# First output projection of a two-layer trunk: six pairs by Strassen products; first chunk's product order and 16 constant matmuls for 20

## The chip, the cores and the metric

The kernel runs on one core of a Trainium2 chip, as one program. The metric is device microseconds of one execution; the kernel before has a median of 2319.4 us over 3 runs (2317.81 to 2319.68). Engines are named as in the profile: PE is the matrix engine (PEld its weight loads), DVE the vector engine, ACT the scalar engine, POOL GpSimd, SP the engine that issues most transfers.

## The reference, cut to what matters

One sequence of 512 tokens with 2048 features goes through two layers. All of it is fp32.

```python
for layer in range(DEPTH):                      # DEPTH = 2
    h = rms_norm(x, norm_pre[layer])
    y = ab_mixer(h, ...) if layer == 0 else conv_mixer(h, ...)   # both end in  y @ w_out, 2048 x 2048
    x = x + rms_norm(y, norm_post[layer])
    h = rms_norm(x, xattn_norm_pre[layer])
    y = memory_cross_attention(h, rms_norm(mem, mem_norm[layer]), ...)
    x = x + rms_norm(y, xattn_norm_post[layer])
```

The change concerns the last line of `ab_mixer`, `return y @ w_out`: a product of 512 x 2048 by 2048 x 2048.

## The kernel before, in words

**Layout.** Activations lie transposed, features on partitions: a tensor of 2048 x 512 is 16 tiles of 128 x 512. `X` (`residual`) holds the residual, `Y` and other scratch lie in `work`. A matmul of full fp32 accuracy is made of three passes: the input is split in a high and a low part (`H_hi`, `H_lo`, together `input_hi_lo`), a weight in `w_hi` and `w_lo`, and hi x hi, hi x lo and lo x hi are summed in PSUM.

**Chunks.** Weights come in chunks of 4 input tiles by 256 output features (128 x 1024, 512 KB). SP loads a chunk to one of 4 slots of `raw`; ACT rounds it to `w_hi` (`split`, L642); DVE subtracts to get `w_lo` (`split`, L1798); PE runs 24 matmuls of 512 columns on it (`chunk`, L1260 to L1262). Four chunks make one pair of output tiles. Counters order all of this: `lo_ready` (weights split), `chunk_used` (PE done with a chunk), `acc_free` (PSUM banks read out).

**First output projection.** `out_phase(0, C_OUT0, P_OUT0, 4)` runs 8 pairs, 32 chunks, with an input split by `split_input` from `X`. The residual `x`, whose place the mixer's result has taken, is loaded again right after that split (16 transfers on semaphore `reloaded`, on SP ahead of the fifth chunk). Sums of squares of each output tile go through ACT and POOL; then `norm(0)` computes the norm, adds the residual and starts the opening of the cross-attention's query projection (`opening`, L1610 to L1623), for which PE waits.

**Strassen pairs.** The second layer's input projection (28 pairs) and output projection (6 of its 8 pairs, `wino_out`) do not use chunks but Winograd's form of Strassen's algorithm: a pair of output tiles takes 7 products instead of 8, each over 8 input tiles and 256 tokens. A product runs 8 matmuls of 512 columns (high and low input side by side, L1757) and 8 of 256 columns (low weights, L1762). Its operands are quarters of the weights and sums of quarters: A11, A12, A22 come from SP by transfer; S1 and S3 from POOL by adding transfers (`wino_sums`, L2807 and L2809); S2 and S4 by DVE additions (`weight_sum`, L2503 and L2506). Sums of input tiles are made beforehand by DVE (`turned_sums_out`, L2688 to L2693), their highs by ACT (L1159), their lows by DVE (`turned_low_out`, L2703). Products are read out of PSUM by DVE and ACT (`evacuate_product`, L2571 to L2598), which PE waits for in products 4 to 7 of a pair. The stage works so: 2 pairs by chunks, meanwhile the input sums; `take_out` copies the two chunk pairs out (L2713, in the first layer L2248); then six pairs by products; meanwhile, in the last pair, the residual returns from DRAM (L610, L613), and `norm(2)` and `opening` follow.

**Start.** While the first transfers are under way, PE runs 20 matmuls on a constant (L1234); then `ab_round(0, 0)` begins with chunk 0.

Of the kernel before, what the change touches and what calls it, by code (L numbers as in the profile page):

```python
# [50 lines left out]
C_Q0, P_Q0 = C_OUT0 + 32, P_OUT0 + 8  # L51
# [138 lines left out]
S_PAIRS, OUT_PAIRS = 28, 6  # L190
S_CHUNKS = 7 * S_PAIRS
S_ALL = 7 * (S_PAIRS + OUT_PAIRS)
# [8 lines left out]
def run_of(q):  # L201

    return (0, S_PAIRS, C_C) if q < S_PAIRS else (S_PAIRS, S_PAIRS + OUT_PAIRS, C_OUT1 - 8)


def s_slot(i):

    return (i + 2) % S_SLOTS
# [11 lines left out]
def build(nc, books, dram):  # L220
    ctx = ExitStack()
    with ctx:
# [19 lines left out]
        gate_pair = sb("gate_hi_lo", KT * 32, F32R)  # L242
        gate_half = lambda n: gate_pair.rearrange("p (k a n) -> p k a n", a=2, n=16)[:, :, n, :]
# [95 lines left out]
        s_s3 = lambda q: raw[:, CW:2 * CW] if q in (0, S_PAIRS) else raw_s3[:, :]  # L339
        home = {"A11": "r0", "S2": "r0", "S1": "r2", "A12": "r1", "S4": "r1", "A22": "r3"}  # L340
        s_source = lambda q, name: s_s3(q) if name == "S3" else s_raw[home[name]][q % 2]
# [5 lines left out]
        fourths_out = lambda b: Y[:, 4 * T:6 * T].rearrange("p (k n) -> p k n", n=HT) if b else four(Y, 8, 0)  # L347
        sq_out = lambda k: (Y[:, (14 + k % 2) * T:(15 + k % 2) * T] if k < 12 else cq[:, (k % 2) * T:(k % 2 + 1) * T])
        out_corner = lambda n, f, h: Y[:, (2 * n + f) * T + h * HT:(2 * n + f) * T + (h + 1) * HT]
        corner = lambda q, f, h: corner_of(q % 4, f, h) if q < S_PAIRS else out_corner(q - S_PAIRS + 2, f, h)  # L350
        before_first, before_second, before_third = (lambda b, k=k, t=t: four(t, 4 * b + k, 1) for k, t in ((0, X), (8, X), (0, Y)))

        def moving(q, pos, kt):

            if pos in (1, 2, 4):
                third = turned_y if q < S_PAIRS else turned_o
# [27 lines left out]
        params_in, consts_in, tables_in, gate_in, reloaded, out_done = (  # L384
            sem(n) for n in ("params_in", "consts_in", "tables_in", "gate_in", "reloaded", "out_done"))
# [38 lines left out]
        def _(sp):  # L424
# [86 lines left out]
            for n in range(8):  # L511
                load_pair(dram["ab_w_out"], 4 * n, C_OUT0 + 4 * n)
                if n == 0:
                    for k in range(KT):
                        sp.wait_ge(*ZV(f"lo{k}"))
                        sp.dma_start(xt(k), dram["x"][k]).then_inc(reloaded, 16)

            def cross_loads(l):
                for c in range(4 * l, 16):
# [4 lines left out]
            cross_loads(0)  # L524
            conv_sections = (0, 2, 1, 3)
            for c in range(16):
                j, kt0 = opening_chunk(c)
                load(dram["c_w_in"], 32 * conv_sections[j] + kt0 // 4, C_C + c)
                if c in (9, 11):
                    for k in range(8 * (c // 11), 8 * (c // 11) + 8):  # L530
                        sp.wait_ge(*(NG(f"x{k}", 1) if k > 1 else NV(f"x{k}", 1)))
                        sp.dma_start(dram["x_kept"][k], xt(k)).then_inc(x_kept, 16)

            def s_load(q, at, home_, sem_):

                if q < S_PAIRS:
                    w, block = dram["c_w_in"], 4 * (8 * conv_sections[q % 4] + q // 4 + 1) + at
                else:
                    w, block = dram["c_w_out"], 4 * (q - S_PAIRS + 2) + at
                sp.dma_start(home_, w[P * block:P * (block + 1), :]).then_inc(sem_, 16)  # L540

            def s_loads(q):

                first, _, base = run_of(q)
# [18 lines left out]
                if q == 0:  # L563
                    sp.wait_ge(*CM("o3", 0))
# [5 lines left out]
                s_load(q, 1, s_raw["r1"][q % 2], s_in["r1", q % 2])  # L570
# [3 lines left out]
                if q:  # L574
                    sp.wait_ge(s_lo, 7 * q)
                s_load(q, 3, s_raw["r3"][0], a22_in)

            def after_pairs(end, c):

                q = end - 2 + c % 2  # L580
                sp.wait_ge(s_lo, 7 * q + (5 if c < 2 else 3))
# [2346 lines left out]
```

## Time and profile before

| | us |
|---|---|
| median of 3 runs | 2319.4 (2317.81 to 2319.68) |
| profiled execution, its own time | 2319.7 |
| span of its profile, first to last instruction | 2317.7 |
| first output projection, `norm(0)`, opening (984.46 to 1212.13) | 227.67 |
| second output projection, `norm(2)`, opening (1975.05 to 2193.22) | 218.17 |

The profile's times count from its first instruction; 2.0 us lie around the span. Stages are bounded by the start of their first matmul. A busy time of PE counts overlapping matmuls once, so a stage's length and the waits ahead of a matmul say more than the share.

### The profile page before, as it was taken

Reading aid. Unit: us, or ns where it says so; the run is one execution under the profiler, and the core shown is the slowest. Engines: PE = TensorE matmul, PEld = TensorE weight load, DVE = VectorE, ACT = ScalarE, POOL = GpSimd, SP = SyncE. Lnnn points to the kernel's source line nnn. Section 1 sums busy time; section 2 is a strip of 40 time slices with the busy share of each in tenths; the row PEclk is TensorE's granted clock in tenths of the full one; section 3 lists DMA queues with packets and bytes.
Section 4 is the critical chain, followed back from the end, with each engine's and each line's share of the span. In section 5 each row is a group of like instructions: output and inputs, shape, how many; then the busy total and the mean of one; then the engine's idle time right before and its main releaser. Section 6 shows DMA issues by size and latency. Waiting matters only on the chain.

```text
span 2317.7 us, 31681 instructions
## 1 busy us (share of the span) xinstructions
PE 2287.0 (99%) x12237; PEld 1919.2 (83%) x12237; DVE 1647.6 (71%) x2240; ACT 985.3 (43%) x1618; POOL 293.8 (13%) x225
## 2 busy tenths in 40 slices
PE   9999999999999999999999899999999999999998
PEld 7888888888787778888877788888888888888776
DVE  6676767664455658643385699888988898988855
ACT  5333333323343437532243364444444444544444
POOL 4000000001010101001040340000000000122400
PEclk9999999999999999999999999999999999999999
DMA  5322222223322224442322245766676666466322
GB/s 209 98 78 82 77 81 77 82 79 99 109 91 73 89 67 156 160 167 84 115 64 72 83 146 172 200 193 190 191 198 179 188 181 201 145 188 204 114 64 91
DMA packets 99553, 297.89 MB, mean 129 GB/s; under 512 B 18624, under 2 KB 21856, under 8 KB 99424
## 3 DMA queue, kind: packets, MB, share of 16 engines
q1 hardware_dynamic: 89152, 258.89, 33.1%
q0 software_dynamic: 9792, 35.66, 8.8%
q8 instruction: 86, 1.41, 0.2%
q10 hardware_dynamic: 480, 1.59, 0.2%
q14 instruction: 43, 0.35, 0.0%
HBM read 285.06 MB, written 11.03 MB: 128 GB/s over the span
## 4 chain that ended last, share of the span: by engine, by line
PE 91%; DVE 5%; issue 2%; ACT 1%; DMA 1%; POOL 0%; DVEq 0%; ACTq 0%; SPq 0%; POOLq 0%
PE acc L1260 15%; PE acc L1262 14%; PE acc L1261 14%; PE m L1757 12%; PE acc L1757 6%; PE m L1762 6%; PE acc L1762 3%; PE acc L1618 2%; PE acc L1619 2%; PE acc L1623 2%; DVE weights_lo L1798 1%; PE m L1434 1%; PE m L1442 1%; ACT weights_hi L642 1%; PE m L1650 1%
## 5 line engine op out<-in xcount | busy, mean ns | idle before, releaser
L1260 PE MATMUL acc<-input_hi_lo,weights_hi 128*128 128x512 f32 (+1 forms) x1696 | 670.8, 395 | 0.8 <-DVE input_hi_lo L2667 0.3
L1262 PE MATMUL acc<-input_hi_lo,weights_lo 128*128 128x512 f32 (+1 forms) x1696 | 648.3, 382 | 0.0
L1261 PE MATMUL acc<-input_hi_lo,weights_hi 128*128 128x512 f32 (+1 forms) x1696 | 647.4, 382 | 0.0
L1798 DVE TENSOR_TENSOR weights_lo<-weights_raw,weights_hi 128x1024 fp32r<-128x1024 f32 x264 | 359.8, 1373 | 134.9 <-ACT weights_hi L642 134.1
L1260 PEld LDWEIGHTS acc<-input_hi_lo,weights_hi 128*128 128x128 f32 x1696 | 319.2, 188 | 72.8 <-issue 14.8
L1262 PEld LDWEIGHTS acc<-input_hi_lo,weights_lo 128*128 128x128 f32 x1696 | 318.8, 188 | 63.9
L1261 PEld LDWEIGHTS acc<-input_hi_lo,weights_hi 128*128 128x128 f32 x1696 | 319.5, 188 | 57.3 <-issue 1.9
L642 ACT ACTIVATE weights_hi<-weights_raw 128x1024 fp32r<-128x1024 f32 x264 | 274.5, 1058 | 144.1 <-PE acc L1262 108.9
L1757 PE MATMUL m<-input_hi_lo,weights_hi 128*128 128x512 f32 x816 | 205.5, 394 | 3.1 <-issue 2.0
L1757 PEld LDWEIGHTS m<-input_hi_lo,weights_hi 128*128 128x128 f32 x816 | 146.6, 189 | 31.3 <-issue 3.9
L1026 ACT ACTIVATE weights_hi<-weights_raw 128x1024 fp32r<-128x1024 f32 x104 | 110.0, 1059 | 112.6 <-PE m L1762 51.9
L2495 DVE TENSOR_TENSOR weights_lo<-weights_raw,weights_hi 128x1024 fp32r<-128x1024 f32 x104 | 128.0, 1231 | 37.6 <-ACT weights_hi L1026 37.6
L2752 POOL TENSOR_TENSOR small<-small 128x4 f32<-128x4 f32 (+1 forms) x19 | 24.5, 1288 | 835.5 <-DVE small L2038 371.6
L1762 PEld LDWEIGHTS m<-input_hi_lo,weights_lo 128*128 128x128 f32 x816 | 111.2, 190 | 8.4 <-DVE weights_lo L2495 0.4
L1762 PE MATMUL m<-input_hi_lo,weights_lo 128*128 128x256 f32 x816 | 113.8, 282 | 0.0
L2495 DVE TENSOR_TENSOR weights_lo<-work,weights_hi 128x1024 fp32r<-128x1024 f32 x68 | 86.6, 1274 | 13.5 <-ACT weights_hi L1026 13.5
L2828 POOL TENSOR_TENSOR work<-work 128x512 f32<-128x512 f32 x42 | 61.0, 1453 | 275.0 <-ACT work L939 197.8
L1026 ACT ACTIVATE weights_hi<-work 128x1024 fp32r<-128x1024 f32 x68 | 71.7, 1055 | 36.9 <-DVE work L2506 36.9
L2807 POOL DMA_DIRECT2D weights_s<-in_c_w_in x27 | 23.7, 879 | 479.8 <-DMA weights_s<-in_c_w_in 479.8
L1618 PE MATMUL acc<-input_hi_lo,weights_hi 128*128 128x512 f32 x180 | 73.5, 408 | 6.6 <-DVE input_hi_lo L2281 6.6
L2838 POOL TENSOR_TENSOR residual<-residual,work 128x512 f32<-128x512 f32 x42 | 71.0, 1713 | 50.9 <-DVE work L2274 50.9
L1619 PE MATMUL acc<-input_hi_lo,weights_lo 128*128 128x512 f32 x180 | 72.7, 404 | 0.0
(403 smaller groups left out, 3638.8 us busy)
## 6 DMA issues: line engine op xcount, KB each, us to landing
weights_raw<-in_ab_w_in SPq DMA_DIRECT2D x126, 512.0 KB, 3.6
weights_raw<-in_c_w_in SPq DMA_DIRECT2D x73, 512.0 KB, 4.5
work<-in_c_w_in SPq DMA_DIRECT2D x42, 512.0 KB, 3.7
weights_raw<-in_m_w_kv SPq DMA_DIRECT2D x32, 512.0 KB, 3.7
weights_raw<-in_ab_w_out SPq DMA_DIRECT2D x32, 512.0 KB, 4.4
weights_raw<-in_m_w_q SPq DMA_DIRECT2D x32, 512.0 KB, 3.6
weights_raw<-in_c_w_in POOLq DMA_DIRECT2D x29, 512.0 KB, 7.5
weights_s<-in_c_w_in SPq DMA_DIRECT2D x27, 512.0 KB, 3.8
```

The source lines that it names most:

```text
L642: act.activation(w_hi[:, s * CW:(s + 1) * CW], raw[:, c * CW:(c + 1) * CW], ACT.Copy)\
L1026: act.activation(w_hi[:, s * CW:(s + 1) * CW], s_source(q, name), ACT.Copy).then_inc(s_hi, 1)
L1260: pe.matmul(out, w_hi[:, o:o + P], hi(kt), start=kt == first_kt, stop=False)
L1261: pe.matmul(out, w_hi[:, o:o + P], lo(kt), start=False, stop=False)
L1262: last = pe.matmul(out, w_lo[:, o:o + P], hi(kt), start=False, stop=kt == last_kt)
L1618: pe.matmul(bank(p0 + n, j), w_hi[:, o:o + P], H_hi[:, x], start=kt == 0, stop=False)
L1619: pe.matmul(bank(p0 + n, j), w_lo[:, o:o + P], H_hi[:, x], start=False, stop=False)
L1757: pe.matmul(out.rearrange("p (a n) -> p a n", a=2), w_hi[:, o:o + P], moving(q, pos, kt)[0], start=kt == 0 and pos in S_FRESH, stop=False, ...
L1762: last = pe.matmul(high_half(out), w_lo[:, o:o + P], moving(q, pos, kt)[1], start=False, stop=kt == 7, skip_group_check=True)
L1798: TTO(w_lo[:, s * CW:(s + 1) * CW], raw[:, c * CW:(c + 1) * CW], w_hi[:, s * CW:(s + 1) * CW].bitcast(F32), ALU.subtract).then_inc(lo_read ...
L2495: TTO(w_lo[:, s * CW:(s + 1) * CW], s_source(q, name), w_hi[:, s * CW:(s + 1) * CW].bitcast(F32), ALU.subtract)\
L2838: pool.tensor_tensor(xt(k), xt(k), yt(k), ALU.add).then_inc(*NG.did(f"x{k}"))
```

## The change

The six last pairs of the first output projection are computed by Strassen products with the code of the second one (`wino_out(r, ...)` is now shared by r = 0 and r = 2, with one function on PE, ACT and DVE each). For that `w_out` is laid out on the host as halves of pairs, the run of products is numbered from 0 (6 here, then 28, then 6), and places are found for quarters where the memory keys and values (`mk`, `mv`) still lie: A12 of even pairs and A22 go to `Y`; from the fifth pair on A22 goes to the place of S1, once S2 has been summed (`late_fourth`). The residual is loaded again late, in the last pair (`residual_back`), no longer ahead of the fifth chunk. In `turned_sums_out` DVE now waits for its first sum before the second, for r = 2 too.

Apart from that, the first chunk of all runs two high products ahead of the low ones and starts before its low weights are there (`first_chunk`), behind 16 constant matmuls.

```diff
-            for k in range(20):
+            for k in range(16):
                 early = pe.matmul(M[3], gate_pair[:, 0:P], gate_pair[:, :], start=True, stop=True)
...
+            def first_chunk():
+                for kt in range(4):
+                    x = slice(kt * T, (kt + 1) * T)
+                    o = [kt * 256 + j * P for j in range(2)]
+                    if kt == 0:
+                        pe.wait_ge(hi_ready, 1)
+                    pe.wait_ge(*SA(f"hi{kt}"))
+                    for j in range(2):
+                        pe.matmul(acc[j][:, :], w_hi[:, o[j]:o[j] + P], H_hi[:, x], start=kt == 0, stop=False)
+                    pe.wait_ge(*SV(f"lo{kt}"))
+                    for j in range(2):
+                        pe.matmul(acc[j][:, :], w_hi[:, o[j]:o[j] + P], H_lo[:, x], start=False, stop=False)
+                    if kt == 0:
+                        pe.wait_ge(lo_ready, 1)
+                    for j in range(2):
+                        last = pe.matmul(acc[j][:, :], w_lo[:, o[j]:o[j] + P], H_hi[:, x], start=False, stop=False)
+                last.then_inc(chunk_used, 1)
...
-S_PAIRS, OUT_PAIRS = 28, 6
+S_FIRST = (0, 6, 34, 40)
+S_BASE = (C_OUT0 - 8, C_C, C_OUT1 - 8)
...
+        def s_home(q, r):
+            if run_of(q) == 0 and r == "r1" and q % 2 == 0:
+                return Y[:, 14 * T:16 * T]
+            if run_of(q) == 0 and r == "r3":
+                return s_raw["r2"][q % 2] if q >= 4 else Y[:, 12 * T:14 * T]
+            return s_raw[r][q % 2]
...
+            def late_fourth(q):
+                sp.wait_ge(s_lo, 7 * q + 3)
+                sp.wait_ge(s_sum["S2"], q + 1)
+                s_load(q, 3, s_home(q, "r3"), a22_in)
...
+            def residual_back(r, c):
+                w, sems = ((dram["x"], (reloaded, reloaded2)) if r == 0 else (dram["x_kept"], (x_back, x_back2)))
+                sp.wait_ge(s_used, 7 * (S_FIRST[r + 1] - 1) + (5 if c else 3))
+                for k in range(8 * c, 8 * c + 8):
+                    sp.dma_start(xt(k), w[k]).then_inc(sems[c], 16)
...
-            for n in range(8):
-                load_pair(dram["ab_w_out"], 4 * n, C_OUT0 + 4 * n)
-                if n == 0:
-                    for k in range(KT):
-                        sp.wait_ge(*ZV(f"lo{k}"))
-                        sp.dma_start(xt(k), dram["x"][k]).then_inc(reloaded, 16)
+            for n in range(2):
+                load_pair(dram["ab_w_out"], 4 * n, C_OUT0 + 4 * n)
+            for q in range(S_FIRST[1]):
+                s_loads(q)
+                if q >= 5:
+                    late_fourth(q - 1)
+            for c in (0, 2):
+                after_pairs(S_FIRST[1], c)
...
+            late_fourth(5)
+            residual_back(0, 0)
+            after_pairs(S_FIRST[1], 1)
...
+            residual_back(0, 1)
+            after_pairs(S_FIRST[1], 3)
...
             def turned_sums_out(r, b):
...
                 TTO(four(third_out, 4 * b, 1), high1, low1, ALU.subtract).then_inc(turn_in, 1)
+                dve.wait_ge(turn_in, 8 * r + 4 * b + 1)
                 TTO(before_first(b), low0, low1, ALU.subtract).then_inc(turn_in, 1)
...
-            out_phase(0, C_OUT0, P_OUT0, 4, lambda kt: ZV(f"lo{kt}", 0))
+            wino_out(0, C_OUT0, P_OUT0, (0, 4, 8, 12), lambda kt: ZV(f"lo{kt}", 0))
             norm(0)
...
-              "ab_w_out": by_block(np.asarray(ab_w_out)[0]), "c_w_in": by_quarter(np.asarray(c_w_in)[0]),
+              "ab_w_out": halves_of_pairs(np.asarray(ab_w_out)[0]), "c_w_in": by_quarter(np.asarray(c_w_in)[0]),
```

On PE, at the program's start, these rows stand in the kernel before (names are those of the tiles, out first; the number behind x counts equal instructions):

```order
L1234 MATMUL m<-gate_hi_lo 128x512 x20
L1260 MATMUL acc<-input_hi_lo,weights_hi 128x512
L1261 MATMUL acc<-input_hi_lo,weights_hi 128x512
L1262 MATMUL acc<-input_hi_lo,weights_lo 128x512
L1260 MATMUL acc<-input_hi_lo,weights_hi 128x512
```

and these after the change:

```order
L1271 MATMUL m<-gate_hi_lo 128x512 x16
L1288 MATMUL acc<-input_hi_lo,weights_hi 128x512 x2
L1291 MATMUL acc<-input_hi_lo,weights_hi 128x512 x2
L1295 MATMUL acc<-input_hi_lo,weights_lo 128x512 x2
L1288 MATMUL acc<-input_hi_lo,weights_hi 128x512 x2
```

The first matmul on the low weights has moved from the third to the fifth place behind the constant ones.

On SP, from the first output projection's loads to those of the next projection, the kernel before has

```order
L434 DMA weights_raw<-in_ab_w_out 128x1024 x4
L516 DMA residual<-in_x 128x512 x16
L434 DMA weights_raw<-in_ab_w_out 128x1024 x28
L434 DMA weights_raw<-in_m_w_q 128x1024 x16
```

and the changed one, from the first quarters of its sixth pair on (L537 loads quarters, L446 chunks of the query projection, L595 the residual),

```order
L537 DMA weights_raw<-in_ab_w_out 128x1024 x2
L537 DMA weights_a_52<-in_ab_w_out 128x1024
L537 DMA weights_s_53<-in_ab_w_out 128x1024
L537 DMA weights_raw<-in_ab_w_out 128x1024
L446 DMA weights_raw<-in_m_w_q 128x1024 x2
L537 DMA weights_raw<-in_ab_w_out 128x1024
L595 DMA residual<-in_x 128x512 x8
L446 DMA weights_raw<-in_m_w_q 128x1024
L595 DMA residual<-in_x 128x512 x8
L446 DMA weights_raw<-in_m_w_q 128x1024 x13
```

The residual has moved from the stage's start to its end, and the query projection's fourth chunk stands behind all of it. The two single `weights_raw<-in_ab_w_out` rows are the late A22 of the fifth and sixth pair.

On DVE, where the first chunk pair is read out, the changed kernel has (L1860 splits weights, L2610 to L2616 are the input sums, L2637 reads out a pair, L2626 makes lows)

```order
L1860 TENSOR_TENSOR weights_lo<-weights_raw,weights_hi 128x1024 x2
L2637 COPY work<-acc 128x512 x2
L2610 TENSOR_TENSOR work<-residual 128x4x256
L2612 TENSOR_TENSOR residual<-residual 128x4x256
L2614 TENSOR_TENSOR residual<-residual 128x4x256
L2616 TENSOR_TENSOR work<-residual 128x1024
L1860 TENSOR_TENSOR weights_lo<-weights_raw,weights_hi 128x1024
L2626 SCALAR_TENSOR_TENSOR turned_third_out<-work,turned_third_out 128x4x256
```

where the kernel before had only the copies (L2248) and the weights' splits (L1798): the second half of the input sums and the lows now stand between the copies and the splits of the seventh and eighth chunk.

## Rows read from the trace of the kernel before

**Rows 1.** The page, parts 1 and 4: busy time, and the chain by engine.

```profile
PE 2287.0 (99%) x12237; PEld 1919.2 (83%) x12237; DVE 1647.6 (71%) x2240; ACT 985.3 (43%) x1618; POOL 293.8 (13%) x225
...
PE 91%; DVE 5%; issue 2%; ACT 1%; DMA 1%; POOL 0%; DVEq 0%; ACTq 0%; SPq 0%; POOLq 0%
```

**Rows 2.** Windows by stage: length, engines' busy time, granted clock, DMA share, GB/s.

```profile
984.46:1159.58 175.12, 175.12 (x780) 145.13 (x778) 64.04 (x60) 47.73 (x58) 18.64 (x15) 1.00 0.36 122
1159.58:1166.17 6.59, 3.06 (x26) 2.81 (x24) 2.89 (x6) 1.23 (x2) 1.02 (x1) 0.90 0.00 0
1166.17:1212.13 45.96, 45.96 (x191) 37.80 (x192) 40.52 (x42) 25.02 (x37) 23.70 (x14) 0.94 0.26 81
1975.05:2018.66 43.61, 43.61 (x192) 36.12 (x193) 41.38 (x44) 22.84 (x30) 5.38 (x4) 1.00 0.42 125
2018.66:2040.83 22.17, 20.25 (x113) 17.23 (x112) 19.41 (x24) 11.05 (x14) 4.84 (x4) 1.00 0.67 174
2040.83:2138.70 97.87, 97.87 (x563) 86.02 (x562) 83.67 (x105) 46.89 (x61) 25.16 (x18) 1.00 0.66 193
2138.70:2148.21 9.51, 5.28 (x35) 4.88 (x33) 5.32 (x9) 2.75 (x5) 1.03 (x1) 0.62 1.05 404
2148.21:2193.22 45.01, 45.01 (x192) 36.94 (x192) 40.51 (x42) 25.04 (x37) 23.68 (x14) 0.97 0.29 96
```

**Rows 3.** PE's timeline, second output projection: sixth and seventh product of its first pair.

```profile
2033.61 2.08 PE L1757 MATMUL m<-input_hi_lo,weights_hi 128*128 128x512 f32 x8 [0.82 <-DVE fifth L2576]
...
2037.96 2.09 PE L1757 MATMUL m<-input_hi_lo,weights_hi 128*128 128x512 f32 x8 [1.09 <-issue]
```

**Rows 4.** Windows of the input projection's first two Strassen pairs, columns as in Rows 2.

```profile
1422.98:1443.64 20.66, 19.78 (x114) 17.26 (x113) 18.66 (x24) 11.32 (x14) 1.79 (x2) 1.00 0.69 195
1443.64:1463.21 19.57, 19.57 (x114) 17.20 (x113) 16.27 (x22) 8.46 (x10) 1.77 (x2) 1.00 0.70 188
```

**Rows 5.** Timelines of DVE and POOL: start, length, operation, idle time ahead.

```profile
1006.56 1.29 DVE L2248 COPY work<-acc 128x512 f32<-128x512 f32 x2 [4.95 <-PE acc L1262]
...
1998.54 1.28 DVE L2713 COPY work<-acc 128x512 f32<-128x512 f32 x2
...
2030.32 1.21 DVE L2506 TENSOR_TENSOR work<-work,weights_raw 128x1024 f32<-128x1024 f32 x1
...
2033.04 0.42 DVE L2576 TENSOR_TENSOR fifth<-m,fifth 128x256 f32<-128x256 f32 x1
...
2037.43 0.43 DVE L2584 SCALAR_TENSOR_TENSOR work<-m,fifth 128x256 f32<-128x256 f32 x1
...
2049.35 2.32 DVE L2506 TENSOR_TENSOR weights_a<-weights_a,weights_raw 128x1024 f32<-128x1024 f32 x1
...
2048.78 1.81 POOL L2828 TENSOR_TENSOR work<-work 128x512 f32<-128x512 f32 x1 [0.47 <-ACT work L1166]
```

**Rows 6.** ACT's timeline: the first pair's S1, and the query chunk split in `norm(2)`.

```profile
2020.92 1.06 ACT L1026 ACTIVATE weights_hi<-weights_raw 128x1024 fp32r<-128x1024 f32 x1 [2.75 <-DMA weights_raw<-in_c_w_out]
...
2151.34 1.05 ACT L642 ACTIVATE weights_hi<-weights_raw 128x1024 fp32r<-128x1024 f32 x1
```

**Rows 7.** Timelines of PE and DVE at the program's start.

```profile
1.47 7.72 PE L1234 MATMUL m<-gate_hi_lo 128*128 128x512 f32 x20 [1.47 <-DVE gate_hi_lo L1802]
9.28 0.50 PE L1260 MATMUL acc<-input_hi_lo,weights_hi 128*128 128x512 f32 x1
...
14.85 0.39 PE L1260 MATMUL acc<-input_hi_lo,weights_hi 128*128 128x512 f32 x1
...
7.13 0.75 DVE L1807 SCALAR_TENSOR_TENSOR input_hi_lo<-residual,parameters,input_hi_lo 128x512 fp32r<-128x512 f32 x1 [5.71 <-ACT input_hi_lo L655]
8.00 1.23 DVE L1798 TENSOR_TENSOR weights_lo<-weights_raw,weights_hi 128x1024 fp32r<-128x1024 f32 x1
```

**Rows 8.** Transfers: quarters with median us to landing; SP's timeline, the residual's issues.

```profile
work<-in_c_w_out SPq DMA_DIRECT2D x9, 512.0 KB, 3.7
...
2133.30 4.33 SPq L613 DMA_DIRECT2D residual<-residual_kept  x8
```

More of the change, by code:

```diff
@@ L587, in _ @@
+            for q in range(S_FIRST[1], S_FIRST[2]):
+                s_loads(q)
+                n, j = divmod(q - S_FIRST[1], 4)
+                if j == 2 and n < 4:
                     sp.wait_ge(*WV("y", n))
@@ L1066, in conv_first @@
                             turned_high(HIGHS_AT[c], n)
-                for i in range(S_SLOTS):
+                for i in range(CONV_I, CONV_I + S_SLOTS):
                     s_split(i)
@@ L1205, in _ @@
-            wino_out()
+            wino_out(2)
             norm(2)
@@ L1718, in last_projection @@
                         turned(k)
-            out_phase(0, C_OUT0, P_OUT0, 4, lambda kt: ZV(f"lo{kt}", 0))
-            norm(0)
-            cross(0, 0)
-            norm(1)
-            def conv_group(n, first=False):
-                if first:
-                    opening(1, C_C, P_C)
-                for c in range(8 if first else 0, 16):
-                    chunk(C_C + c, P_C + c // 4, 4 * (c % 4), KT - 1, n=n,
-                          between=(lambda k: next_rms(1, c, k)) if first else None)
-            conv_group(0, first=True)
             def wino_product(q, pos):
@@ new lines, in _, with turned_sums @@
+            split_input(0, xt, C_OUT0, 8)
+            wino_out(0)
+            norm(0)
+            cross(0, 0)
+            norm(1)
+            def turned_sums(b):
+                (low0, low1), (high0, high1) = ([four(X, 4 * b + k, h) for h in range(2)] for k in (0, 8))
+                dve.wait_ge(turn_scaled, 8 * (b + 1))
+                TTO(before_third(b), high1, low1, ALU.subtract).then_inc(turn_in, 1)
+                TTO(before_first(b), low0, low1, ALU.subtract).then_inc(turn_in, 1)
+                dve.wait_ge(turn_in, 8 + 4 * b + 2)
+                TTO(before_second(b), high1, before_first(b), ALU.add).then_inc(turn_in, 1)
+                dve.wait_ge(turn_in, 8 + 4 * b + 3)
+                TTO(fourths(b), before_second(b), high0, ALU.subtract).then_inc(turn_in, 1)
@@ new lines, in turned_low @@
+            def turned_low(b):
+                for n in (2, 0, 1):
+                    of = (before_first, before_second, before_third)[n](b)
+                    home_, k = (turned_y if n == 2 else turned_x), 4 * b + (0, 8, 0)[n]
+                    dve.wait_ge(turn_hi, 8 + 3 * b + (2, 0, 1).index(n) + 1)
+                    STT(out=four(home_, k, 1), in0=of, scalar=-1.0 if n == 1 else 1.0,
+                        in1=four(home_, k, 0).bitcast(F32), op0=ALU.mult, op1=ALU.subtract).then_inc(turn_lo, 1)
@@ L2841, in _ @@
                 if r == 1:
-                    for q in range(S_PAIRS):
+                    for q in range(S_FIRST[1], S_FIRST[2]):
                         wino_sums(q)
```

571 lines of the change are left out of this document (290 added, 281 removed).

## The prediction

> **What bounds the kernel now.** I read the profile's page first: PE is busy for 99% of the span and carries 91% of the chain that ended last [rows 1]. So a stage lasts as long as its matmuls follow each other plus the waits ahead of them, and an edit off PE counts only where PE comes to wait for it. Then I cut both output projections into windows by stage [rows 2]; they are the same product of the same size, one by chunks and one by Strassen pairs, so the second is a measured model of what the first is to become. In the first, eight chunk pairs take 175.12 us (21.89 each, PE without a gap), the norm 6.59 and the opening of the query projection 45.96: together 227.67. In the second, two chunk pairs take 43.61, the first Strassen pair 22.17, the other five 97.87 (19.57 each), the norm 9.51 and the opening 45.01: together 218.17.
>
> Next I looked for what makes the first Strassen pair longer than the others by 22.17 - 19.57 = 2.60 us. PE's timeline shows it: the sixth product waits 0.82 us for DVE's second addition for the fifth term (L2576), the seventh 1.09 [rows 3], the rest being gaps too short to be listed as waits. DVE's row L2576 ends at 2033.46, just ahead of the sixth product, and its row L2584 at 2037.86, just ahead of the seventh [rows 5]. DVE is late there because that pair's S1 came late: ACT split it only at 2020.92, after 2.75 us of waiting for its transfer [rows 6], and from then on DVE works through splits, additions and the second copy without rest. The input projection's first pair loses less: 20.66 - 19.57 = 1.09 us [rows 4].
>
> **The change part by part.**
>
> *Six pairs by products.* Six of the eight pairs go from 21.89 to 19.57 us. With the second projection's parts put in for the first's, the stage is 43.61 + 6 x 19.57 + 9.51 + 45.01 = 215.55 plus what the first pair waits. Against 227.67 that is a gain of 12.12 us less that wait. The longer norm (9.51 for 6.59) is inside the sum: 24 columns of sums of squares now follow the last product, where the old loop put 8 of them between the last chunk's matmuls; and the opening is 0.95 us shorter in the second projection, at a granted clock of 0.97 for 0.94 [rows 2]. I take both as they stand, since the changed kernel has the same steps in the same order there.
>
> *The first pair's wait.* It lies between nothing, as in the five pairs that follow, and the model's 2.60; the input projection's first pair, with 1.09, stands between. Which is nearest? The chain to S1 starts where DVE has copied out the first chunk pair and makes the second half of the input sums. In the first projection that copy came 1006.56 - 984.46 = 22.10 us after the stage's first matmul, in the second 1998.54 - 1975.05 = 23.49 [rows 5], because DVE had a backlog there from the step before. So the chain can start 1.4 us earlier. Not all of that arrives at S1: in the first projection ACT's third high waits for all four sums, so that the squares that POOL adds ahead of its weight sums come about 1 us later than in the model, and the transfers share the engines (0.67 of them busy in that window [rows 2]). I take 1.1 us of the 1.4, hence a wait of 1.5 us.
>
> *DVE and POOL beside each other.* In the Strassen pairs DVE makes its additions while POOL adds squares. The row for S4 shows what that costs: 1.21 us at 2030.32, and 2.32 at 2049.35, while POOL's addition runs from 2048.78 for 1.81 [rows 5]. So an overlapped addition loses 1.11 us, and with two POOL additions a pair DVE loses some 2.2; it has 19.57 - 83.67 / 5 = 2.84 us free in a pair with these losses already in it [rows 2], so PE loses nothing. The Trainium skill's page "SBUF — State Buffer" (section "SBUF: two separate sides") speaks against the change here: a VectorE operation with two SBUF inputs and a GpSimd operation that reads SBUF take the same port pair as an exclusive lock, and the later one waits for the whole of the other. Two full waits of 1.81 in place of 1.11 would take 1.4 us more from DVE's free 2.84, so by that rule too the sum stays as it is.
>
> *A22 at a new place, and late for two pairs.* For the first four pairs A22 is asked for as in the model. For the fifth and sixth it takes the place of S1, so SP may ask for it only when S1 has been split and S2 summed. One product is 19.57 / 7 = 2.80 us; I estimate 3 us from the pair's start for that. With the median landing of 3.7 us for such quarters [rows 8] it is there at 6.8. Its split is needed by the seventh product, at 6 x 2.80 = 16.8, so about 15.7 would still do. Cost nothing, covered by some 9 us; behind it on SP stand the query chunks and the residual, which are not needed before the norm.
>
> *The residual's return.* It now competes with nothing at the stage's start, where PE waited for nothing anyway; worth nothing. At the end it returns as in the model, where transfers fill the engines through the norm (1.05, 404 GB/s [rows 2]). Two things differ: the 1 MB of gain rows of the model is not loaded here, and the query projection's fourth chunk stands behind the last eight residual tiles. In the model SP issues those eight from 2133.30 for 4.33 us [rows 8]; the chunk would follow at 2137.7 and land, at 404 GB/s behind 2 MB of them, by about 2145. ACT splits it at 2151.34 in the model [rows 6]. Cost nothing, covered by 6 us; if that cover were gone, ACT's highs for the opening would be queued behind it and PE would wait for them.
>
> *One more wait on DVE in the shared sums*, for r = 2 too: it keeps two additions of the last block from overlapping by about 0.1 us each, on the same chain to S1. Between 0 and 0.3; I take 0.15 lost.
>
> *The first chunk.* PE ends the 20 constant matmuls at about 9.0 and starts chunk 0 at 9.28, when DVE's low weights, 1.23 us from 8.00, are done; chunk 1 starts at 14.85, so 24 matmuls take 5.57, 0.232 each [rows 7]. DVE begins these low weights at 8.00 because the high ones are ready then, and the first input's low part is done at 7.13 + 0.75 = 7.88. With 16 constant matmuls PE is free at about 8.1, four matmuls of the first tile fit ahead of 9.28, and 20 are left: 9.28 + 20 x 0.232 = 13.92, a gain of 0.93. The third tile's low part comes just in time, for which I take off 0.1: 0.85. Bounds: 0 if PE meets a wait later that absorbs it, 1.15 if all from 8.1 on is used. PE is without longer gaps from there to the projection, so I let the gain run through.
>
> Sum: 12.12 - 1.5 - 0.15 + 0.85 = 11.3 us. Against the profiled execution's 2319.7 that is 2308.4; this execution lay 0.3 above the median, so I forecast **2308.1 us**.
>
> **The rivals.**
>
> *The first pair waits as in the model, and the first chunk's gain is small.* For it: the chain to S1 is bound by transfers, which do not care for DVE's earlier start. Against: the copy's 1.4 us. Time: 12.12 - 2.60 - 0.3 + 0 to 0.85 = 9.2 to 10.1 gained, 2309.3 to 2310.2. Chance 0.25.
>
> *A transfer is late.* Either A22 in the last two pairs, if it lands more than 9 us after my estimate, or the fourth query chunk or the residual after the norm. For it: the queue is fuller than in the model's pairs, and POOL's adding transfers go through the same engines. Against: 6 and 9 us of cover. Four us of lateness on A22 count twice: 2316; a chunk late by 3 us gives 2311. Chance 0.12.
>
> *DVE becomes the bound of the Strassen pairs: slower.* Each pair has 2.84 us of DVE to spare; the stage's gain is about 2 us a pair. From 2.84 + 2.02 = 4.9 us more of DVE a pair the change costs time. That needs five more of its some nine long operations a pair to be stretched by 1.11 us. If all nine were, a pair took some 26 us and the kernel 2347. For it: overlapped additions do double. Against: POOL is busy for 25.16 of 97.87 us in the model [rows 2], and the changed stage has the same POOL work. Chance 0.04. (It is what the rule of the Trainium skill's page "SBUF — State Buffer", named above, would come to if every long operation met one of POOL's.)
>
> *The pairs gain nothing,* because halves of 256 columns run no better here than chunks: 2319. Against: 19.57 us a pair both in the second output projection's last five and in the input projection's second [rows 2, 4]. Chance 0.04.
>
> **How the numbers follow.** The forecast case has 0.55. The range 2305.8 to 2312.0 holds it with its bounds (no wait in the first pair and a first chunk of 1.15 give 13.27 us and 2306.1; I add 0.3 for the spread between executions), all of the second case and a third of the late transfers: some 0.85. A measurement of this kernel can tell about 0.2%, 4.6 us, from no change. Faster by more than that (below 2314.8): the first two cases and most of the third, 0.91. Same: 0.05. Slower: 0.04.
>
> **What would show it.** In the changed kernel's profile, Strassen pairs two to six of the first projection should take 19.6 us each, the first one 20.5 to 22, PE's wait there ahead of the sixth or seventh product and named after DVE; the norm some 9.5 us and the opening 45. Chunk 1 should start near 13.9. The prediction is wrong if PE waits ahead of a seventh product in the fifth or sixth pair (A22), if ACT waits for a transfer in `norm(0)`, or if DVE is busy through whole pairs.

## The result, and the profile after

The changed kernel takes 2307.4 us (median of 5 runs, 2307.04 to 2309.31), the kernel before beside it 2319.7 (5 runs): a ratio of 0.995, 95% interval 0.9936 to 0.9964. The forecast was 2308.1, the range 2305.8 to 2312.0. The total is right; in the profile two of its terms came out smaller than forecast, and the account below weighs them against the scatter between profiles.

The profile after: span 2305.5, 12.24 us less than before. The stage windows that answer to [rows 2] (times, then busy times of PE, PEld, DVE, ACT and POOL, granted clock, DMA share, GB/s): the first output projection's two chunk pairs, first Strassen pair, other five, norm and opening, the stretch from there to the next opening; then the second projection's first pair and its other five.

```profile
983.88:1027.51 43.63, 43.63 (x195) 36.13 (x194) 36.26 (x36) 20.62 (x26) 6.26 (x5) 1.00 0.46 144
1027.51:1049.39 21.88, 20.24 (x113) 17.23 (x112) 18.64 (x23) 11.09 (x14) 4.58 (x4) 1.00 0.60 165
1049.39:1147.25 97.86, 97.86 (x562) 86.00 (x561) 83.78 (x105) 46.70 (x60) 24.52 (x18) 1.00 0.66 191
1147.25:1156.77 9.52, 5.32 (x34) 4.93 (x33) 5.31 (x9) 2.96 (x5) 1.03 (x1) 0.62 0.94 367
1156.77:1201.70 44.93, 44.93 (x192) 36.91 (x192) 40.44 (x42) 25.04 (x37) 23.60 (x14) 0.97 0.26 82
1201.70:1320.51 118.81, 112.74 (x514) 91.50 (x513) 72.13 (x80) 45.77 (x82) 21.53 (x17) 0.97 0.24 76
...
2006.91:2028.64 21.73, 20.26 (x114) 17.23 (x113) 19.09 (x24) 11.15 (x14) 4.40 (x4) 1.00 0.66 177
2028.64:2126.50 97.86, 97.86 (x562) 86.01 (x561) 83.65 (x105) 46.55 (x60) 24.95 (x18) 1.00 0.65 192
```

The one stretch of before that [rows 2] lack:

```profile
1212.13:1331.90 119.77, 113.70 (x514) 92.48 (x513) 72.13 (x80) 45.77 (x82) 21.51 (x17) 0.96 0.24 75
```

So the 12.24 us are made of: 0.58 at the start (the stage begins at 983.88 for 984.46); 9.85 in the stage, 217.82 for 227.67 (pairs 175.12 to 163.37, norm 6.59 to 9.52, opening 45.96 to 44.93); 0.96 in the stretch behind it (119.77 to 118.81), which the change does not touch; and 0.85 in what remains, 0.44 of it in the second projection's first pair (22.17 to 21.73).

PE's timeline in the first pair shows the model's two waits again, ahead of the sixth and the seventh product:

```profile
1042.18 2.09 PE L1804 MATMUL m<-input_hi_lo,weights_hi 128*128 128x512 f32 x8 [0.55 <-DVE fifth L2579]
...
1046.52 0.70 PE L1804 MATMUL m<-input_hi_lo,weights_hi 128*128 128x512 f32 x2 [1.09 <-issue]
```

DVE's first copy, POOL's timeline to S1's issue (L2878 is S3's adding transfer, L2880 S1's), ACT's split of S1 and DVE's low split of it:

```profile
1005.95 1.29 DVE L2637 COPY work<-acc 128x512 f32<-128x512 f32 x2 [4.51 <-PE acc L1318]
...
1013.85 1.72 POOL L2899 TENSOR_TENSOR work<-work,squares 128x512 f32<-128x512 f32 x1 [22.30 <-ACT squares L1096]
1015.71 2.10 POOL L2899 TENSOR_TENSOR work<-work,rstd_rows 128x512 f32<-128x512 f32 x1
1017.75 1.05 POOL L2878 DMA_DIRECT2D weights_raw<-in_ab_w_out  x1
1018.50 1.22 POOL L2880 DMA_DIRECT2D weights_raw<-in_ab_w_out  x1
...
1029.49 1.06 ACT L1053 ACTIVATE weights_hi<-weights_raw 128x1024 fp32r<-128x1024 f32 x1 [4.11 <-DMA weights_raw<-in_ab_w_out]
...
1030.58 1.23 DVE L2551 TENSOR_TENSOR weights_lo<-weights_raw,weights_hi 128x1024 fp32r<-128x1024 f32 x1 [3.94 <-ACT weights_hi L1053]
```

The copy comes 22.07 us after the stage's first matmul, as forecast; S3 is issued 33.87 after it, S1's split starts at 45.61. In the second projection of before these were 23.49, 34.03 and 45.87 (S3's issue there at 2009.08, the rest from [rows 5, 6]): of the 1.4 us gained at the copy 0.2 to 0.3 reach S1 in this profile. DVE is idle for 3.94 us ahead of S1's low split, so it is S1, and not S3 (split at 1024.32) or DVE's own earlier work, that DVE waits for.

At the start PE's timeline reads

```profile
8.21 0.73 PE L1288 MATMUL acc<-input_hi_lo,weights_hi 128*128 128x512 f32 x2 [0.67 <-ACT weights_hi L676]
8.78 0.63 PE L1291 MATMUL acc<-input_hi_lo,weights_hi 128*128 128x512 f32 x2
9.47 0.73 PE L1295 MATMUL acc<-input_hi_lo,weights_lo 128*128 128x512 f32 x2
...
14.33 0.39 PE L1316 MATMUL acc<-input_hi_lo,weights_hi 128*128 128x512 f32 x1
```

Four matmuls stand ahead of the low weights, as forecast, but these came at 9.47 (9.28 in [rows 7]), since the first input landed later in this execution: ACT's first high starts at 6.49 (6.30 before).

### The profile page after: what moved, and what is told of

Read it like the earlier page. It is cut to its first block, busy times and chain, and to the rows that moved or that the text cites. A ratio compares the mean times of both kernels' runs of the same rounds, so it can differ in the third digit from the quotient of the medians.

```text
span 2305.5 us, 32170 instructions
## 1 busy us (share of the span) xinstructions
PE 2271.9 (99%) x12329; PEld 1911.9 (83%) x12329; DVE 1724.5 (75%) x2346; ACT 1018.2 (44%) x1662; POOL 308.6 (13%) x237
## 3 DMA queue, kind: packets, MB, share of 16 engines
q0 software_dynamic: 11520, 41.95, 10.4%
## 4 chain that ended last, share of the span: by engine, by line
PE 88%; DVE 6%; issue 2%; ACT 2%; DMA 1%; POOL 1%; DVEq 0%; ACTq 0%; SPq 0%; POOLq 0%
PE m L1804 14%; PE acc L1316 13%; PE acc L1318 12%; PE acc L1317 12%; PE acc L1804 7%; PE m L1809 7%; PE acc L1809 4%; PE acc L1677 2%; PE acc L1678 2%; PE acc L1682 2%; DVE weights_lo L1860 1%; PE m L1490 1%; PE m L1498 1%; ACT weights_hi L676 1%; PE m L1709 1%
## 5 line engine op out<-in xcount | busy, mean ns | idle before, releaser
L1316 PE MATMUL acc<-input_hi_lo,weights_hi 128*128 128x512 f32 (+1 forms) x1504 | 595.9, 396 | 0.7 <-DVE input_hi_lo L2797 0.3
L1318 PE MATMUL acc<-input_hi_lo,weights_lo 128*128 128x512 f32 (+1 forms) x1504 | 573.6, 381 | 0.0
L1317 PE MATMUL acc<-input_hi_lo,weights_hi 128*128 128x512 f32 (+1 forms) x1504 | 572.7, 381 | 0.0
L1860 DVE TENSOR_TENSOR weights_lo<-weights_raw,weights_hi 128x1024 fp32r<-128x1024 f32 x240 | 324.3, 1360 | 84.3 <-ACT weights_hi L676 83.6
L1316 PEld LDWEIGHTS acc<-input_hi_lo,weights_hi 128*128 128x128 f32 x1504 | 283.2, 188 | 64.8 <-issue 14.8
L1318 PEld LDWEIGHTS acc<-input_hi_lo,weights_lo 128*128 128x128 f32 x1504 | 282.7, 188 | 56.4
L1317 PEld LDWEIGHTS acc<-input_hi_lo,weights_hi 128*128 128x128 f32 x1504 | 283.5, 188 | 49.8 <-issue 1.9
L1804 PE MATMUL m<-input_hi_lo,weights_hi 128*128 128x512 f32 x960 | 241.5, 393 | 4.4 <-issue 3.1
L1804 PEld LDWEIGHTS m<-input_hi_lo,weights_hi 128*128 128x128 f32 x960 | 172.6, 189 | 37.4 <-issue 6.4
L2822 POOL TENSOR_TENSOR small<-small 128x4 f32<-128x4 f32 (+1 forms) x19 | 24.5, 1290 | 822.8 <-DVE small L2100 371.6
L1809 PE MATMUL m<-input_hi_lo,weights_lo 128*128 128x256 f32 x960 | 134.0, 282 | 0.0
L2878 POOL DMA_DIRECT2D weights_s<-in_c_w_in x27 | 23.6, 872 | 480.1 <-DMA weights_s<-in_c_w_in 480.1
L1804 PE MATMUL acc<-turned_first,weights_hi 128*128 128x512 f32 x320 | 80.1, 392 | 0.0
L1804 PE MATMUL m<-turned_first,weights_hi 128*128 128x512 f32 x320 | 80.1, 392 | 0.0
L1804 PE MATMUL acc<-input_hi_lo,weights_hi 128*128 128x512 f32 x320 | 80.1, 392 | 0.0
L1677 PE MATMUL acc<-input_hi_lo,weights_hi 128*128 128x512 f32 x180 | 73.3, 408 | 6.7 <-DVE input_hi_lo L2343 6.7
```

What stands on the lines that cost most here:

```text
L1316: pe.matmul(out, w_hi[:, o:o + P], hi(kt), start=kt == first_kt, stop=False)
L1317: pe.matmul(out, w_hi[:, o:o + P], lo(kt), start=False, stop=False)
L1318: last = pe.matmul(out, w_lo[:, o:o + P], hi(kt), start=False, stop=kt == last_kt)
L1677: pe.matmul(bank(p0 + n, j), w_hi[:, o:o + P], H_hi[:, x], start=kt == 0, stop=False)
L1804: pe.matmul(out.rearrange("p (a n) -> p a n", a=2), w_hi[:, o:o + P], moving(q, pos, kt)[0], start=kt == 0 and pos in S_FRESH, stop=False, ...
L1809: last = pe.matmul(high_half(out), w_lo[:, o:o + P], moving(q, pos, kt)[1], start=False, stop=kt == 7, skip_group_check=True)
```

## The experiments

All but one are edits of the changed kernel. First pairs and starts are read from the profiles, whose resolution the medians do not have.

**Both weight sums ahead of the squares** (POOL, both output projections).

```diff
-                    if r in (0, 2) and k == 2:
+                    if r in (0, 2) and k == 0:
                         wino_sums(S_FIRST[r])
```

> Edit: on POOL, in both output projections, the first pair's two weight sums (S3, S1) stand ahead of the first two additions of squares, no longer behind them. Theory 'queue' (the first pair waits because S1's adding transfer is issued behind POOL's two additions, which wait for ACT's squares and those for DVE's input sums): S3 is issued as soon as its base quarter has landed, near 1005 in place of 1017.75, S1 as soon as its own has, near 1016.8 in place of 1018.5, and without S3 ahead of it lands near 1022 to 1024 in place of 1029.5; the first pairs shrink from 21.88 and 21.73 to 19.6 to 20.6 us, the kernel gains 2 to 4 us more: 2303.5 to 2305.5. Theory 'transfers' (the transfer engines set the landing, whatever the issue): S1 lands within 1 us of where it did, first pairs 21.4 or more, kernel 2306.5 to 2308. Theory 'DVE' (its own backlog of splits and lows sets the wait): S1 lands early but the pairs stay above 21.2 us.

2304.4 us (5 runs, 2303.22 to 2305.63; ratio to before 0.9936, interval 0.9923 to 0.995). Windows of the two first pairs:

```profile
1027.29:1046.84 19.55, 19.55 (x113) 17.19 (x112) 18.07 (x23) 10.33 (x13) 5.50 (x4) 1.00 0.65 176
2004.46:2024.01 19.55, 19.55 (x113) 17.22 (x112) 17.94 (x23) 11.40 (x14) 5.76 (x5) 1.00 0.63 163
```

POOL's timeline, and ACT's split of S1:

```profile
1005.19 1.06 POOL L2878 DMA_DIRECT2D weights_raw<-in_ab_w_out  x1 [13.87 <-DMA weights_raw<-in_ab_w_out]
1016.96 0.88 POOL L2880 DMA_DIRECT2D weights_raw<-in_ab_w_out  x1 [10.71 <-DMA weights_raw<-in_ab_w_out]
...
1025.91 1.06 ACT L1053 ACTIVATE weights_hi<-weights_raw 128x1024 fp32r<-128x1024 f32 x1 [5.95 <-DMA weights_raw<-in_ab_w_out]
```

The wait is gone in both projections: the pairs take what the later ones take. DVE's backlog alone falls as a cause, since its work is the same. But S1 came only 1.5 us earlier to its issue and 3.6 earlier to its split, at 1025.91, later than the 1022 to 1024 that 'queue' had forecast: the issue is not all of it.

**S3 alone ahead of the squares**, S1 behind them as before.

```diff
-                    if r in (0, 2) and k == 2:
-                        wino_sums(S_FIRST[r])
+                    if r in (0, 2) and k in (0, 2):
+                        wino_sums(S_FIRST[r], (k // 2,))     # part 0: S3, part 1: S1
```

> The changed kernel with only S3 of the first pair ahead of POOL's two additions of squares; S1 stays behind them. Moving both gave first pairs of 19.55 us, but with that S1 was issued 1.5 us earlier and its landing took 8.9 us in place of 11.0. If the place behind the squares is what made PE wait: S1 issued near 1018 again, first pairs 20.5 us or more. If S3's half megabyte ahead of S1 in the transfer queue is what made it late: S1 lands 8 to 9 us after its issue, near 1026.5, first pairs 19.5 to 20.2.

POOL's issue of S1 and ACT's split of it:

```profile
1017.52 0.90 POOL L2883 DMA_DIRECT2D weights_raw<-in_ab_w_out  x1
...
1024.19 1.06 ACT L1053 ACTIVATE weights_hi<-weights_raw 128x1024 fp32r<-128x1024 f32 x1 [4.34 <-DMA weights_raw<-in_ab_w_out]
```

First pairs 19.55 and 19.55, with S1 issued behind the squares again, 6.67 us ahead of its split; in the changed kernel that distance is 10.99, and 9.7 to 10.4 in three other profiles with this code unchanged. So S1 is late because S3's transfer starts right ahead of it; the squares matter in that they hold S3 back until S1's base is there too. Whether the two delay each other by the order of their queue or by sharing the engines was not separated. Nor is it shown why S1's distance was 8.95 us with both sums ahead, where S3 was as early as here. Timed as a run of its own:

> The changed kernel with S3 alone ahead of POOL's additions of squares, timed. Its one look gave first pairs of 19.55 us and 2304.06; if that is the whole of the first pairs' waits, 2303.3 to 2305, the same as with both sums ahead (2304.44), and 2.5 to 4 us under the changed kernel's 2307.42.

2304.5 us (5 runs, 2303.92 to 2306.39; ratio 0.9935, interval 0.9921 to 0.9948), first pairs 19.55 again. Either order of POOL beats both kernels, the changed one by 3 us with no run in common.

**The seventh chunk's low split ahead of the input sums** (DVE).

```diff
-                turned_sums_out(r, 1)
                 split(c0 + 6)
+                turned_sums_out(r, 1)
```

> Edit: on DVE, in both output projections, the seventh chunk's low split stands ahead of the second half of the input sums, no longer behind it; POOL as it was. The base quarter of S1 is asked for some 4.9 us earlier (near 1008.4 for 1013.3), the input sums come 1.2 us later. Theory 'queue' (POOL's additions of squares, behind the input sums, hold S1 back): S1 is issued some 1.2 us later than now (near 1019.7) and lands no earlier than 1029; first pairs 21.6 to 23 us. Theory 'transfers' (late base quarters and their traffic hold S1 back): S1 lands 2 us or more earlier, first pairs 19.6 to 20.8.

S1 issued at 1019.36, split at 1028.51; first pairs 21.21 and 21.49, below the range of 'queue' and above that of 'transfers'. The early base quarter does not free the pair. Counted from the stage's start S1 was split 0.7 us earlier than in the changed kernel, although it was issued 1.1 later; but three profiles whose code is unchanged here show 0.6, 0.7 and 1.3 us earlier too, so a part of the quarters' traffic in the wait is not shown.

**The added DVE wait only for r = 0.**

```diff
-                dve.wait_ge(turn_in, 8 * r + 4 * b + 1)
+                if r == 0:
+                    dve.wait_ge(turn_in, 8 * r + 4 * b + 1)
```

> Edit: DVE's added wait between its first and second input sum only in the first output projection, in the second as before the change. The second projection's first pair took 22.17 us before the change and 21.73 with it. If the wait costs what the prediction gave it (0.15 us on the chain to S1): 21.5 to 21.65. If the wait is what made that pair shorter: 22.1 to 22.3. If both numbers are scatter of the transfers from execution to execution: anything from 21.4 to 22.4, with S1's issue at the same distance from the stage's start within 0.2 us.

21.97 us; and the first projection's first pair, whose code is untouched, 21.33 for 21.88. The scatter of these pairs (below) is larger than the effect that was looked for. S1's issue tells more: without the added wait it comes 34.62 us after the stage's first matmul, as in the kernel before (34.63), and with it 34.86 to 35.09 in five profiles. So the wait costs 0.2 to 0.5 us at S1's issue; at S1's split (45.69, beside 45.43 to 46.21 in those five) this is lost in the scatter.

**The first chunk alone**, put in the kernel before.

> The kernel before with the first chunk's new order and 16 constant matmuls alone. If the first chunk's gain runs through: chunk 1 starts 0.5 to 0.75 us ahead of 14.85, the first output projection starts as much ahead of 984.46, and the kernel gains 0.5 to 0.8 us: 2318.6 to 2319.2 beside 2319.4. If a later wait absorbs it: 0 to 0.2. The 0.96 us that the changed kernel gained between the opening and the second norm (the granted clock fell later there, in the norm before the next projection): if it comes from the Strassen stage's end, that stretch stays at 119.8 us here; if it varies from execution to execution, it may show 118.8 here too.

Chunk 1 starts at 14.28 (14.85 before), and the rows stay 0.6 to 0.7 us ahead up to the first norm. In this execution that norm took 7.51 us, beside 6.59 in the kernel before, whose code there is the same; the opening behind it began 0.2 us later than before. The opening takes 45.96 us, as in the kernel before, and the stretch behind it 119.67 (119.77 before). Norm and stretch:

```profile
1158.84:1166.35 7.51, 3.98 (x26) 3.63 (x24) 2.89 (x6) 1.23 (x2) 1.02 (x1) 0.66 0.00 0
1212.31:1331.98 119.67, 113.60 (x514) 92.49 (x513) 72.02 (x80) 45.64 (x82) 21.54 (x17) 0.96 0.25 75
```

The granted clock of the norm is 0.66, in the kernel before 0.90 [rows 2]. The median is 2318.5 (11 runs) for 2319.6; ratio 0.9996, interval 0.9987 to 1.0005: a time can't tell the first chunk's gain.

**20 constants with the new order; 16 with the old order; and a further order** in which the second tile's highs fill the wait for the low weights (with POOL's early sums).

```diff
-            for k in range(16):
+            for k in range(20):
                 early = pe.matmul(...)
```

> The changed kernel with 20 constant matmuls again, the first chunk's new order kept. If the gain of 0.5 to 0.6 us needs both parts: PE ends the constants at 9.0, goes straight on with 24 matmuls, chunk 1 starts at 14.5 to 14.7. If the order alone brings it: 14.2 to 14.35.

> The changed kernel with the old order of the first chunk behind 16 constant matmuls. If the low weights' readiness sets the start: the first matmul waits to 9.3 to 9.5 and chunk 1 starts at 14.8 to 15.1, no gain or a small loss. If the granted clock falls in the wait of nearly 2 us: matmuls of 0.43 us, chunk 1 after 15.5.

> Both weight sums ahead of the squares, as in the earlier run, and in the first chunk the second tile's two high products ahead of the first tile's low-weight products, which wait for DVE. Chunk 1 starts 0.2 to 0.35 us earlier than with the changed kernel's order (13.85 to 14.05 beside 14.03 to 14.33), first pairs 19.55 both, the kernel 2303.5 to 2305 beside 2304.4 for the sums alone; if the second tile's input lows then wait instead, no gain at the start.

PE's timelines at the start, of the 20 constants, the old order and the further order:

```profile
1.47 6.55 PE L1271 MATMUL m<-gate_hi_lo 128*128 128x512 f32 x20 [1.47 <-DVE gate_hi_lo L1864]
8.13 0.72 PE L1288 MATMUL acc<-input_hi_lo,weights_hi 128*128 128x512 f32 x2
...
14.25 0.39 PE L1316 MATMUL acc<-input_hi_lo,weights_hi 128*128 128x512 f32 x1
```

```profile
9.47 0.50 PE L1316 MATMUL acc<-input_hi_lo,weights_hi 128*128 128x512 f32 x1 [1.46 <-DVE weights_lo L1857]
...
15.06 0.39 PE L1316 MATMUL acc<-input_hi_lo,weights_hi 128*128 128x512 f32 x1
```

```profile
11.80 0.73 PE L1290 MATMUL acc<-input_hi_lo,weights_hi 128*128 128x512 f32 x2 [0.15 <-DVE input_hi_lo L1880]
...
14.20 0.39 PE L1327 MATMUL acc<-input_hi_lo,weights_hi 128*128 128x512 f32 x1
```

Fewer constants alone gain nothing (15.06 for 14.85, the low weights 0.19 later). The order alone brings the gain where the 20 constants end in time; they did here, at 8.02, while in the kernel before they ended at 9.19 [rows 7], because matmuls took up their fast pace earlier: from 5.3 to 6.4 us six of them run, in the kernel before four (the granted clock reads 1.00 in both, so the pace is read from the count). Sixteen keep the gain in either case. The further order trades the wait at 9.3 for one at 11.8 for DVE's third input low and gains nothing: 2305.8 us (5 runs), no better than the early sums by themselves and above the forecast 2303.5 to 2305. That low part is the next bound of the start.

**Two and four more DVE operations a pair** (r = 0; low splits made twice).

```diff
                 dve.wait_ge(s_hi, i + 1)
+                if run_of(q) == 0 and i % 7 in (1, 4):          # the other run: (0, 1, 3, 4)
+                    TTO(w_lo[...], s_source(q, name), w_hi[...], ALU.subtract).then_inc(twice, 1)
+                    dve.wait_ge(twice, ...)
                 TTO(w_lo[...], s_source(q, name), w_hi[...], ALU.subtract).then_inc(s_lo, 1)
```

> The changed kernel with two more DVE operations of 128 x 1024 in every Strassen pair of the first output projection (the low splits of A11's and the fifth operand's places made twice, some 1.2 us each). DVE is idle 2.8 us of a pair of 19.57. If free time in a pair is what counts, as the prediction took it: pairs two to six stay at 19.57 to 19.9, kernel 2306 to 2309. If the place counts (an operation that stands ahead of a product's read-out delays PE at once): pairs of 20 us and more.

> The same with four more operations a pair, some 4.9 us: more than the 2.8 free. By the prediction's rival (DVE becomes the bound once 2.84 us more are asked of it) pairs two to six grow by what is over, 1.9 to 2.6 us each, to 21.5 to 22.2, and the Strassen pairs' gain over the chunks' 21.89 is used up; kernel 2315 to 2320. If DVE is not near being the bound: below 20 us a pair.

Windows of pairs two to five: with two more, with four more, and of the changed kernel:

```profile
1048.68:1130.31 81.63, 79.22 (x451) 69.03 (x450) 76.05 (x93) 37.09 (x48) 20.36 (x16) 1.00 0.67 183
```

```profile
1050.23:1140.40 90.17, 80.90 (x450) 68.99 (x449) 86.75 (x101) 37.53 (x48) 19.80 (x16) 1.00 0.61 166
```

```profile
1049.39:1127.68 78.29, 78.29 (x450) 68.81 (x449) 67.42 (x85) 37.54 (x48) 20.88 (x16) 1.00 0.69 190
```

A pair goes from 19.57 to 20.41 and 22.54 us; the kernels take 2311.9 and 2324.4 (one run each). With two, DVE is busy 2.2 us more in a pair and still has 1.4 idle, and yet each pair is 0.8 longer: not all of DVE's free time can be used. With four, the products are slower than the chunks' 21.89, and slower than the 21.5 to 22.2 that was expected.

**S1's split and PE's wait, over the profiles.** For the first pairs, whose DVE work is the same in all of these: the time from the stage's first matmul to ACT's split of S1, and behind the colon what the pair takes beyond 19.57 us.

| profile | first projection | second projection |
|---|---|---|
| kernel before | (chunks) | 45.87: 2.60 |
| changed kernel | 45.61: 2.31 | 45.43: 2.16 |
| added DVE wait only for r = 0 | 45.05: 1.76 | 45.69: 2.40 |
| seventh low split first | 44.93: 1.64 | 45.19: 1.92 |
| 20 constants | 44.95: 1.66 | 46.12: 2.86 |
| old order, 16 constants | 44.30: 1.00 | 46.02: 2.78 |
| two and four more DVE operations (r = 0 only) | (other work) | 45.94: 2.68; 46.21: 2.96 |
| S3 or both sums early, four profiles | 40.53 to 42.25: 0 | 42.62 to 43.96: 0 |

In the thirteen pairs that wait, the wait is S1's split less 43.24 to 43.30: PE's wait follows S1's lateness one for one. DVE passes it on: in the changed kernel it has no listed idle time from S1's low split (1030.58) to its addition ahead of the seventh product (L2587, which ends at 1046.41). Two operations in that chain are stretched by POOL's additions, to 2.31 and 2.21 us from 1.2, so the overlap that costs the later pairs nothing is on PE's path here. The line must not be drawn on below 44.3: with both sums early S1's split came at 43.96 in the second projection and PE met no wait; there the second overlap cost DVE 0.3 us in place of 1.0.

## Why the prediction was right, and where it was not

**Six pairs by products: right.** 43.63 + 19.57 + 97.86 = 161.06 us without the first pair's wait, forecast 161.03; norm and opening 54.45 together, forecast 54.52.

**The first pair's wait: 21.88 - 19.57 = 2.31 us in this profile, for 1.5 (1.65 with the DVE wait).** One profile does not show that the term was mis-sized: the three others with this pair's code unchanged have 1.00, 1.66 and 1.76 us, and the forecast lies among them. What fell short in this execution is the step "I take 1.1 us of the 1.4": 0.26 us reached S1 here, against 0.82, 0.92 and 1.57 in the other three. The prediction named the loss itself (ACT's third high waits for all four sums). What it did not see is what makes S1 late, the order in POOL's queue: S3, whose base had long landed (POOL could issue it at 1005.19), was held back with S1 and stood right ahead of it. This comes nearest to the first rival's "bound by transfers". It was in the model too, so the model's wait carried it into the forecast unseen.

**The first chunk: 0.58 us in this profile, for 0.85.** The mechanism held. Of the difference 0.19 is the later landing in this execution; the pair of matmuls right behind the wait for the low weights takes 0.73 us (9.47 above; 0.63 at 8.78), which the sum left out. In the eight other profiles with this order and 16 constants the stage begins 0.71 to 0.91 us ahead of 984.46, so the size held as well. The prediction read the end of the 20 constants as 9.0; by [rows 7] it is 1.47 + 7.72 = 9.19. The sum does not change by that, since four matmuls still fit ahead of 9.28; the bound of 1.15 comes down to some 1.0.

**A22 and the residual: right.** The last pair's A22 was issued 3.79 us after the pair's start (forecast 3), and PE met no wait there. The query chunks came so:

```profile
1131.47 0.33 SPq L537 DMA_DIRECT2D weights_raw<-in_ab_w_out  x1
1136.28 3.65 SPq L595 DMA_DIRECT2D residual<-in_x  x8
...
1146.10 3.72 SPq L446 DMA_DIRECT2D weights_raw<-in_m_w_q  x3
...
1146.42 1.06 ACT L676 ACTIVATE weights_hi<-weights_raw 128x1024 fp32r<-128x1024 f32 x1 [3.48 <-DMA weights_raw<-in_m_w_q]
```

ACT waited 3.48 us for the query projection's second chunk, up to 1146.42. That is 0.8 us ahead of the norm's first matmul, so the prediction's sign against itself, such a wait in `norm(0)`, did not come about, if narrowly; PE's opening starts at 1156.77, and the second projection of before has the same wait (3.29 us, up to 2137.66), so it cost nothing. The fourth chunk, the first of the three issued from 1146.10 on, was split at 1159.90 with no wait for a transfer.

**DVE beside POOL: right for this kernel, the bound too generous.** No pair after the first lost time. The rival's point of reversal was 4.9 us more of DVE a pair; by the two runs (20.41 us at 2.2 more, 22.54 at 4.8) a pair is 2.02 us longer, the gain that the rival set against it, near 3.6, an estimate on the line between them. Its 26 us for a pair with all nine operations stretched counts two of them twice, since the 16.73 us of DVE in a pair hold two overlaps already; with seven more it is 24.5 us, and the kernel some 2338 in place of 2347. The Trainium skill's page "SBUF — State Buffer" (section "SBUF: two separate sides") has the later of the two engines wait for the whole of the other's instruction. The rows agree where POOL began first. Here DVE's operation, 1.21 us without an overlap, ends at 1044.16, 1.08 after POOL's:

```profile
1041.95 2.21 DVE L2551 TENSOR_TENSOR weights_lo<-work,weights_hi 128x1024 fp32r<-128x1024 f32 x1
...
1041.80 1.28 POOL L2899 TENSOR_TENSOR work<-work,rstd_rows 128x512 f32<-128x512 f32 x1 [3.91 <-ACT rstd_rows L1096]
```

One row, in the last section, differs: there DVE began first by the profile and waited all the same.

**The total was partly lucky.** By its own terms the change brought 9.85 + 0.58 = 10.43 us, 0.9 less than the forecast's 11.3. The rest of the 12.24 came from two places with no term: 0.96 behind the opening and 0.85 later. Neither is shown to belong to the change. The same kernel (S3 alone ahead) showed both lengths of the first stretches in its two profiles (opening and what follows, to the next opening):

```profile
1154.21:1215.23 61.02, 60.91 (x268) 50.23 (x269) 54.45 (x53) 27.37 (x39) 25.99 (x16) 0.97 0.25 79
1215.23:1317.82 102.59, 96.64 (x439) 78.10 (x438) 58.11 (x68) 43.48 (x79) 19.16 (x15) 0.97 0.24 77
```

```profile
1154.22:1216.18 61.96, 61.84 (x269) 50.94 (x269) 54.58 (x53) 27.34 (x39) 26.11 (x16) 0.95 0.25 78
1216.18:1320.05 103.87, 97.91 (x439) 79.41 (x438) 58.10 (x68) 43.44 (x79) 19.12 (x15) 0.95 0.23 76
```

That is 163.61 and 165.83 us at a granted clock of 0.97 and 0.95. The second projection's first pair took 21.73 to 22.53 us in the profiles that have its code as in the changed kernel, so the 0.44 won there is within scatter too. From the opening's start to that of the next opening the two kernels with chunks took 165.73 and 165.63 us (before, and the first chunk alone); of the eleven profiles with Strassen pairs here eight took 163.5 to 164.0, and three 165.5 to 165.8. The opening's 1.03, which the forecast had in its model, is part of that difference. So the new stage may make the shorter form likelier, but two profiles with chunks are too few to show it. The norm of 6.59 us, from which the forecast counted, is one execution's too: the same code took 7.51 with the first chunk alone.

## What to carry to other kernels

Where the same product exists twice in a kernel, the stage that already has the new form is the best model, its waits included: what is taken off such a wait needs each link of the chain behind it, and one profile of it carries a scatter of a microsecond. In a queue that runs in order, look at what stands directly ahead of the late transfer and ask why that was not issued earlier. A difference between two profiles in stretches that the change does not touch has to be held against two profiles of one kernel before it is counted. The same holds for a term of a microsecond or two: on one profile two terms of this forecast looked mis-sized, and over several they are not.

## What was not expected of the hardware

A long DVE operation that starts ahead of POOL's addition can wait for it as well. In the run with the old first chunk order the S4 addition began 0.48 us ahead of POOL's and took 3.52 us, ending 1.09 after POOL's end (POOL was then issuing an adding transfer, from 1096.35 for 1.21 us, but beside such an issue alone, from 1034.29 for 1.24 in the changed kernel, a DVE operation took the usual 1.22); it is the only one of the runs' pairs two to five, outside the runs with added DVE work, where this reached PE: 20.45 us for that pair.

```profile
1096.44 3.52 DVE L2559 TENSOR_TENSOR weights_a<-weights_a,weights_raw 128x1024 f32<-128x1024 f32 x1
...
1096.92 1.95 POOL L2896 TENSOR_TENSOR work<-work,squares 128x512 f32<-128x512 f32 x1
```

First pairs whose own code was the same took from 20.57 to 21.88 us in the first projection: S1's split scatters between 44.30 and 45.61 us behind the stage's start from execution to execution, and PE's wait follows it.
